# A ring of twelve weight slots instead of six in the first routed layer of a two-block transformer forward pass

## The reference, cut to what matters

```python
def _grouped_moe(x, router_w, router_b, w1, w3, w2):
    ...
    gates = sel / jnp.sum(sel, axis=-1, keepdims=True)
    gate_dense = jnp.sum(jax.nn.one_hot(expert_idx, N_EXPERTS, dtype=jnp.float32) * gates[..., None], axis=1)
    out = jnp.zeros_like(xt)
    for e in range(N_EXPERTS):
        hid = jax.nn.silu(xt @ w1[e]) * (xt @ w3[e])
        out = out + gate_dense[:, e, None].astype(xt.dtype) * (hid @ w2[e])
    return out.reshape(b, s, d)
```

## Time and profile before

| | |
|---|---|
| median of 3 runs | 2496.35 us (2494.48 to 2502.24) |
| the profiled execution: its own time, its span | 2497.97 us, 2496.2 us |
| mean granted clock of TensorE | 0.947 of full speed |
| busy over the span | PE 90%, DVE 63%, ACT 50%, POOL 4% |
| moved by DMA | 592 MB, 237 GB/s over the span |
| first routed layer, from its first weight load issued to its last addition | 338.9 to 640.5 us |

### The profile page before, as it was taken

One profiled execution on the slowest core, in us unless ns is written; L12 is line 12 of the kernel. 1 busy time (PEld: TensorE's weight loads), 2 busy tenths in 40 slices (PEclk: granted clock), 3 DMA queues, 4 the chain that ended last, 5 costly groups with the idle time before them and its releaser, 6 DMA issues.

```text
span 2496.2 us, 31567 instructions
## 1 busy us (share of the span) xinstructions
PE 2250.2 (90%) x12508; PEld 1791.1 (72%) x12508; DVE 1580.0 (63%) x1887; ACT 1255.6 (50%) x1370; POOL 109.0 (4%) x89
## 2 busy tenths in 40 slices
PE   8998898998788888998798699999999999999994
PEld 7887783333667678997557577777778787878773
DVE  4546651221425666775176588878888888888885
ACT  3554431111333554432284477676767676767672
POOL 3002000000000002230000000000000000000000
PEclk9999978999888999998799699999999999999997
DMA  8530436999723134555402499999989998989892
GB/s 268 160 125 1 152 135 253 418 416 403 220 90 119 60 125 140 174 185 155 119 1 85 163 358 340 334 338 324 348 320 353 327 364 317 367 306 368 309 363 87
DMA packets 285683, 592.16 MB, mean 237 GB/s; under 512 B 12124, under 2 KB 118016, under 8 KB 277249
## 3 DMA queue, kind: packets, MB, share of 16 engines
q1 hardware_dynamic: 280000, 571.54, 64.7%
q0 software_dynamic: 5568, 19.06, 2.5%
HBM read 589.45 MB, written 1.11 MB: 237 GB/s over the span
## 4 chain that ended last, share of the span: by engine, by line
PE 71%; DMA 11%; ACT 8%; DVE 7%; issue 2%; SPq 0%; POOL 0%; DVEq 0%; ACTq 0%; POOLq 0%
PE psF L1039 9%; PE psF L1041 9%; PE psF L1040 9%; PE psB L1039 8%; PE psB L1040 8%; PE psB L1041 8%; DMA ring<-in_w_dram 4%; DMA ring<-in_moe_w_gate_dram 4%; PE psF L1399 2%; PE psB L1421 2%; ACT arena_rounded L1848 2%; PE psB L1094 2%; PE psB L1266 1%; ACT ring_rounded L1680 1%; PE psF L1232 1%
## 5 line engine op out<-in xcount | busy, mean ns | idle before, releaser
L1848 ACT ACTIVATE arena_rounded<-ring 128x2048 fp32r<-128x2048 f32 x224 | 429.5, 1919 | 194.5 <-DMA ring<-in_moe_w_up_dram 133.3
L2391 DVE TENSOR_TENSOR ring_rounded<-ring,arena_rounded 128x2048 fp32r<-128x2048 f32 x224 | 507.1, 2286 | 29.2 <-ACT arena_rounded L1848 28.3
L1039 PE MATMUL psF<-arena_rounded 128*128 128x512 f32 x896 | 359.9, 402 | 4.4 <-DVE arena_rounded L2404 1.6
L1041 PE MATMUL psF<-arena_rounded 128*128 128x512 f32 x896 | 354.8, 396 | 0.0
L1040 PE MATMUL psF<-ring_rounded,arena_rounded 128*128 128x512 f32 x896 | 354.0, 395 | 0.0
L2088 DVE TENSOR_TENSOR ring_rounded<-ring,ring_rounded 128x2048 fp32r<-128x2048 f32 (+1 forms) x71 | 153.8, 2170 | 174.0 <-ACT ring_rounded L1680 173.8
L1039 PEld LDWEIGHTS psF<-arena_rounded 128*128 128x128 f32 x896 | 169.6, 189 | 45.1 <-issue 5.7
L1041 PEld LDWEIGHTS psF<-arena_rounded 128*128 128x128 f32 x896 | 169.2, 189 | 39.6
L1040 PEld LDWEIGHTS psF<-ring_rounded,arena_rounded 128*128 128x128 f32 x896 | 169.6, 189 | 37.6
L1040 PE MATMUL psB<-ring_rounded,PT_rounded 128*128 128x512 f32 x448 | 178.5, 398 | 0.0
L1680 ACT ACTIVATE ring_rounded<-ring 128x2048 fp32r<-128x2048 f32 (+1 forms) x71 | 128.4, 1811 | 86.8 <-PE psF L1041 60.7
(11 more groups left out here) (401 smaller groups left out, 4680.3 us busy)
## 6 DMA issues: line engine op xcount, KB each, us to landing
ring<-in_moe_w_gate_dram SPq DMA_DIRECT2D x112, 1024.0 KB, 5.2
ring<-in_moe_w_up_dram SPq DMA_DIRECT2D x112, 1024.0 KB, 5.1
ring<-in_moe_w_down_dram SPq DMA_DIRECT2D x112, 1024.0 KB, 4.9
ring<-in_w_dram SPq DMA_DIRECT2D x96, 1024.0 KB, 9.0
ring<-in_w_in_dram SPq DMA_DIRECT2D x14, 1024.0 KB, 5.4
ring<-in_ff_w_gate_dram SPq DMA_DIRECT2D x11, 1024.0 KB, 7.3
ring<-in_ff_w_up_dram SPq DMA_DIRECT2D x11, 1024.0 KB, 9.7
ring<-in_ff_w_down_dram SPq DMA_DIRECT2D x11, 1024.0 KB, 5.0
```

Source lines behind the costliest of these rows:

```text
L1039: mm(bank, x1, w1, start=start, stop=False, skip_group_check=open_groups)
L1041: return mm(bank, x2, w1, start=False, stop=stop, skip_group_check=open_groups)
L1848: ap_(w_hi[slot].bitcast(R32), ring[:, slot], ACT.Copy).then_inc(q["high"], 1)
L2391: V.tensor_tensor(ring_r[:, slot].bitcast(R32), ring[:, slot], w_hi[slot], ALU.subtract)\
```

## The change

The first routed layer gets a ring of twelve slots (`layer.ring = RING * group`): the six of `ring`, then `memT`, `mv` and four in `arena`. `place` gives each of the 96 pieces its number in the order of use, and the slot is that number modulo 12. The first six loads wait as before; the next six wait until "mem1 out" is finished; every later one waits for the use of the piece twelve places before. The numbers in `freed` for the next stage change with the slots: its first four loads now wait for pieces 84 to 87 of the layer (the up parts of the last unit), where before two of them waited for pieces of the last down part. The second routed layer keeps six slots.

```diff
+        self.ring = RING * group
...
+    def place(self, n, i):
+        gates, all_ = 4 * self.group, 6 * self.group
+        return i if n == 0 else gates + all_ * (n - 1) + (i if n < self.n else i - gates)
...
+        more_slots = [v[:].rearrange("p a b -> p (a b)") for v in (memT, mv)] + \
+            [Region(1536 + SLOT * i).get(SLOT) for i in range(4)]
+        def raw(slot):
+            return ring[:, slot, :] if slot < RING else more_slots[slot - RING]
...
-            layer.q["w_in"] = [sem(f"{name}_weights_in{i}") for i in range(RING)]
+            layer.q["w_in"] = [sem(f"{name}_weights_in{i}") for i in range(layer.ring)]
...
+                freed[len(chunks) - 1] = (layer.q["used"], layer.n * len(layer.every) - layer.ring + i + 1
+                                          if layer.per == 1 else
+                                          layer.nth(layer.every, 0, layer.n - (not down), at, "last" if down else "in"))
...
+                def load_raw(u, n, i):
+                    place, w = layer.place(n, i), views[i // layer.group // 2]
+                    slot = place % layer.ring
+                    if place >= layer.ring or not (isinstance(r, int) and r == 0):
+                        past_use = r * layer.n * len(layer.every) + (place - layer.ring + 1)
+                        sp.wait_ge(layer.q["used"], past_use)
+                    elif slot < RING:
+                        sp.wait_ge(*freed[held_before[layer.first + slot]])
+                    else:
+                        sp.wait_ge(res_ready, add_span("mem1 out")[1])
+                    src = w[u * layer.group + i % layer.group, i // layer.group % 2]
+                    sp.dma_start(raw(slot).rearrange("p (a n) -> p a n", a=src.shape[1]), src)\
+                        .then_inc(layer.q["w_in"][slot], 16)
...
-                    if not layer.split:
-                        pe.wait_ge(q["w_in"][slot], layer.nth(layer.in_slot(i), r, n, i, where) * 16)
-                        return (ring[:, slot],)
+                    if not layer.split:
+                        place = layer.place(n, i)
+                        slot = place % layer.ring
+                        pe.wait_ge(q["w_in"][slot], (r * layer.n + (place // layer.ring + 1)) * 16)
+                        return (raw(slot),)
```

More of the change, by code:

```diff
@@ L505, in routed @@
                 chunks.append((None, 0, 0))
-                freed[len(chunks) - 1] = (layer.q["used"], layer.nth(layer.every, 0, layer.n - (not down), at,
-                                                                     "last" if down else "in"))
+                freed[len(chunks) - 1] = (layer.q["used"], layer.n * len(layer.every) - layer.ring + i + 1
+                                          if layer.per == 1 else
+                                          layer.nth(layer.every, 0, layer.n - (not down), at, "last" if down else "in"))
         transposes("mem1 transposed", mem_tok, memT)
@@ L839, in load_round @@
             def load_round(layer, views, r):
+                def load_raw(u, n, i):
[11 more added lines that the diff above has]
+                        .then_inc(layer.q["w_in"][slot], 16)
                 def load(u, s, n, i, where):
+                    if layer.per == 1:
+                        load_raw(u, n, i)
+                        return
                     e, part, slot = u * layer.group + i % layer.group, i // layer.group, i % RING
@@ L849, in load @@
                         sp.wait_ge(*freed[held_before[layer.first + i % RING]])
[L850 to L854, removed]
+                    src = views[part // 2][bass.ds(e, 1), s, part % 2].rearrange("e p a n -> p (e a) n")
                     sp.dma_start(ring[:, slot, :].rearrange("p (a n) -> p a n", a=src.shape[1]), src)\
```

## The result

The kernel with twelve slots took 2477.85 us in the median of 10 runs, the kernel before 2502.2 us in 10 runs beside them. The ratio is 0.9914, with a 95% interval of 0.9895 to 0.9932: 21.5 us faster (17.0 to 26.3). The ratio is not simply that of the two medians, which lie 24.35 us apart; that gain, too, is inside the interval. The kernel before came out 5.85 us above the median of the three runs shown ahead. The forecast gain taken from its new median would give 2502.2 - 23.55 = 2478.7 us.

The account below looks back on a forecast made before the run. DMA paces the first routed layer by a small margin (30.1 against 28.05 us a unit), after an idle stretch. -22.9 + 0.85 - 1.5 + 0.5 - 0.5 = -23.55 us gives 2473 us; range 2468 to 2482.

Parts of the forecast that it names:

- The mechanism: First routed layer: six more pieces load early in DMA's idle stretch, removing 22.9 us of PE's waits for weights.
- When each piece lands: First routed layer: after reloading starts at 391.01, one piece per 2.51 us; piece 91 lands at 594.6, piece 95 at 604.6.
- the first rival: First routed layer: DMA rate gives way a little, 2.61 us a piece, gain about 17 us, 2479 us; chance 0.13.
- the slower one: First routed layer: DMA rate falls as in other stretches, 3.0 us a piece, 2511 us; chance 0.02.
- When PE wants it: First routed layer, waits removed, copy and clock corrected: PE wants piece 91 at 594.5 and piece 95 at 606.6.
- The remaining waits: First routed layer: waits for weights still left because landings and PE's wants just meet, +0.5 us, between 0 and +2.3.
- The wait for DVE's copy: Unit change at 405 us: PE's wait for DVE's copy of turned token rows, hidden before, appears, +0.85 us.
- The clock: Behind the former 3.79 us wait at the unit change: granted clock no longer falls, -1.5 us, bounds 0 and -1.5.
- its sign of being right: First routed layer: among the signs named for a right forecast, the clock stays 1.00 from 392 us on.
- The jump: Layer's end, 4.61 us over unused rounds: shorter as next stage's loads land before it, -0.5 us, between 0 and -1.1.
- What lies behind the layer: Next stage and all that follows: only moves forward, put at nothing.
- a rival of 0.07 in which a part is given back: After the layer: loads meet in another order or clock falls elsewhere; half the gain lost, 2482 to 2490; chance 0.07.

## Why the prediction was right

The forecast was 2473 us in 2468 to 2482; 2477.85 came out, and the gain was 21.5 us (24.35 between the medians) where 23.55 were predicted. By its steps:

**The mechanism** held: twelve loads before 348 us, DMA busy until 376 us (381 forecast, with a first load 2.9 us later), no wait for weights until the seventh of the eight units, a unit at PE's pace. The two experiments that undo a part show it: without the head start the waits return to 16.4 us, and with two slots more instead of six they are 12.2. Two readings in it were wrong and cost nothing. What ran until 366 us in the kernel before was the memory input that POOL loads at 359.42; the sixth piece had landed at 360.5. And piece 91 is not an up piece but a down piece of the seventh unit, as its line, 1421, says.

**When each piece lands.** This was forecast a little too early. The loads go on when PE has used its first piece, at 384.16 now and at 391.01 in the kernel before. Counted from there, piece 91 let PE go on 205.1 us later (589.23); the forecast was 594.6 - 391.01 = 203.6. That is 1.5 us in some 80 pieces, or 2.53 us a piece instead of 2.51. So the first rival, 2.61 us a piece, did not come about, and neither did the slower one. The Trainium skill, "HBM Reference", specifications, has about 425 GB/s for a core that streams alone; the unit windows, at 417, are near that and far from its 358.

**When PE wants it.** In the profile of twelve slots PE wanted piece 91 at 587.75, 207.2 us after its first product, where the forecast has 210.0. But those 2.7 us are the clock at the layer's start: the first 48 products took 10.52 us there and 13.35 in the trace that the forecast was made from. The profile with the next stage's loads late is the same kernel up to here and starts at half clock:

```profile
381.08 13.35 PE L1428 MATMUL psF<-ring,arena 128*64 128x512 f32 x48 [0.83 <-issue]
...
592.57 0.61 PE L1450 MATMUL psB<-memT,PT 128*64 128x512 f32 x1 [1.46 <-DMA mv<-in_w_dram]
```

Here PE wanted the piece at 591.11, 210.0 us after its first product, to the tenth what was forecast, and had it at 211.5 where 210.1 was forecast. That the first number agrees is luck. It contains three waits that the forecast did not have, 2.8 us with 0.5 us of cost beside their length; without them PE would have been there after 206.7 us. So the forecast of PE's own pace was 3.3 us too slow. The step took PE's floor from a unit that had waits in it, 28.05 us. A lone group of 16 instructions takes 3.65 us, but 32 without a pause take 7.09, not 7.30. Two fewer waits brought the unit to 27.69: each wait costs its length and 0.18 us more. Nineteen such waits stood ahead of piece 91, which makes 3.4 us.

**The remaining waits** were mis-sized: +0.5 us, at most 2.3, was forecast, and 4.2 us were measured. The two reasons are the ones above: PE is faster by 3.3 us, so it uses up the head start sooner, and the pieces land 1.5 us later. The first of them hardly moves the end of the layer, since that goes by the last landings either way.

**The wait for DVE's copy** came as forecast: the pause behind the turned rows is 0.83 us (0.85 forecast).

**The clock** stayed at 1.00 behind the first unit, and the 32 instructions took 7.09 us, where it was 8.78: -1.7 us against -1.5. But it fell in another place, between the last two scatters: 13.50 us there, where the kernel before took 12.68 with a wait of 0.54 inside. Without that wait and its 0.18 these are 11.96, so the fall cost 1.5 us. None of the five profiles of the kernel before has it. The prediction had not looked there; with its sign of being right, a clock of 1.00 from 392 us on, it was wrong. What brings the fall stays open.

**The jump** got 0.56 us shorter in the mean, from 5.12 to 4.56 us, and 0.5 was forecast. The run with late loads shows that its ground was right, but the agreement is partly luck: the forecast started from 4.61 us, the shortest of the five jumps of the kernel before, and so expected 4.1; no profile came below 4.42, and between the two profiled executions the gain is 0.04 us. Nor does a run show that it reaches the total.

For the layer in the two profiled executions the sum is: waits -18.7, per-wait cost -2.9, clock behind the first unit -1.7, clock at the layer's start -2.8 (both starts occur in either kernel), copy +0.8, clock in the tail +1.5. That is -23.8 us, as measured, and the nearness to the forecast holds some chance: with like starts the layer gained 22.3 to 22.7 us.

**What lies behind the layer.** I had put it at nothing, with a rival of 0.07 in which a part is given back. From before to now the profiled execution was ahead by 27.8 us at the layer's end, 26.7 us at the layer norm ahead of the second routed layer, and 20.0 us at the end. The first of these holds the 4.0 us by which the first gate product came earlier; 2.9 of them were there before the first extra load, and the rest is the clock in the stretch before the layer (0.63 and 0.50 in the windows from 370 us). The loss lies in the second routed layer, whose window was then

```profile
1352.51:2463.95 1111.44, 1042.70 (x4552) 834.86 (x4552) 889.53 (x595) 734.79 (x513) 1.05 (x2) 0.97 0.89 318
```

In the kernel before the same stretch of the program was

```profile
1379.18:2483.93 1104.75, 1040.88 (x4552) 833.96 (x4552) 889.53 (x595) 734.88 (x513) 1.05 (x2) 0.97 0.90 320
```

The instructions in it are the same. What differs is how long ScalarE waits for weights: 326.2 us in all now, 319.4 before. Over the profiles the length was 1097.8 to 1104.8 us for the kernel before (mean of five 1101.2) and 1106.6 to 1111.4 for twelve slots (mean of three 1109.3), but 1098.8 to 1110.2 in six profiles with some other change to the ring or its loads, two of them with twelve slots (1103.7 and 1105.1). The first two repeats of the kernel before, 1100.5 and 1101.5 us, came out below both of their expected ranges (1103 to 1106 for a cost, 1104 to 1112 for scatter). The last two, 1097.8 and 1101.1, and the third profile of twelve slots, 1106.6, are what a cost would give; the two others with twelve slots speak against one. The timed runs show no such loss: over the eight timed comparisons the gains add up to 171.3 us, and layer and jump alone account for 176.5, so 0.65 us for each kernel is missing. Whether twelve slots cost a few us there, and by what, stays open.

## What to carry to other kernels

Where a stage is paced by its loads by a small margin and DMA is idle just before it, size the ring by both: the margin times the number of units is the head start that is wanted, and one slot is worth one transfer until it is reached. Then take PE's floor from a unit without waits, since every wait costs more than its length, so the head start has to be reckoned from the faster unit. Release the next stage's loads early enough that they do not run all through a jump over skipped code. And before two traces are compared, look whether the clock stood alike at the start of the stretch.

## What the runs showed of the hardware

- A pause of PE for weights costs about 0.18 us more than it lasts: a unit without waits took 27.69 us, with two of 2.03 us in all 30.08.
- Behind two pauses of 1.48 and 1.79 us, 6 us apart, the granted clock stood at 0.72 and 0.85 over 4 us each (means over the levels 1.00 and 0.50, which are 2.4 and 1.2 GHz) and the stretch took 1.5 us longer; behind the same two pauses it stayed at 1.00 in four other profiles. The pauses do not decide it alone. The Trainium skill, "TensorE: Matmul & The Clock Gate", Part 1, says that the clock gate's phase is free-running, so that one kernel differs from run to run; the starts of the layer, 10.52 or 13.35 us in the same kernel, agree with it, and for the tail it would be an explanation that no run here proves.
- The jump over unused code took 4.4 to 4.6 us when the loads landed before it or up to 2.4 us into it (once 4.90), 4.6 to 5.6 us at 2.7 to 3.7 us, and 7.75 us at 9.8. DMA carries packets of the kind "instruction"; the one of 16 KB in the jump started 1.9 us behind the layer's end when the queue was empty and 5.0 us when it was full, and PE worked 2.5 to 3.0 us after that start in all fourteen profiles. What fills the queue ahead of this packet was varied in one run only.
- Transfers at 417 instead of 228 GB/s into the buffers beside those that PE reads did not lengthen its unit by a hundredth of a microsecond.
